# Squares of the late output tiles moved from VectorE to ScalarE, and their sum to TensorE, in a two-layer hybrid diffusion block

## The reference

```python
def rmsnorm(x, g):
    xf = x.astype(jnp.float32)
    y = xf * lax.rsqrt(jnp.mean(xf * xf, axis=-1, keepdims=True) + RMS_EPS)
    return (y * g.astype(jnp.float32)).astype(x.dtype)
...
y = jnp.concatenate([y_gla, y_four, y_conv], axis=-1) @ w_out
x = x + mod_lat[2] * rmsnorm(y_lat, g_mix_post[i])
...
h = modulate(rmsnorm(x, g_pre), shift, scale)
a, u = jnp.split(h @ w_ffn_in, 2, axis=-1)
y = (jax.nn.silu(a) * u) @ w_ffn_out
return x + gate * rmsnorm(y, g_post)
```

## Time and profile before

| what | value |
|---|---|
| median of 3 runs | 1631.08 us (1630.3 to 1632.72) |
| the profiled execution's own time | 1628.16 us |
| its span | 1626.4 us |
| TensorE busy | 1550.0 us, 95% of the span |
| VectorE busy | 845.3 us, 52% |
| ScalarE busy | 568.3 us, 35% |
| GpSimd busy | 589.6 us, 36% |

### The profile page before, as it was taken

How to read it: one execution, slowest core, us unless ns; L and a number is a source line. 1 busy time by engine, 2 the same in 40 slices (tenths; PEclk the granted TensorE clock), 3 DMA queues, 4 the chain that set the end, 5 groups by cost and what they waited for, 6 DMA issues and landing times.

```text
span 1626.4 us, 23073 instructions
## 1 busy us (share of the span) xinstructions
PE 1550.0 (95%) x9124; PEld 1385.0 (85%) x9124; DVE 845.3 (52%) x1361; ACT 568.3 (35%) x917; POOL 589.6 (36%) x309
## 2 busy tenths in 40 slices
PE   5998999999899999999999979999989999999997
PEld 2898999786799999999998769888877888888886
DVE  2576887746756326661466764366645321221137
ACT  4643214525444214441243255422424422231221
POOL 0531212245324524552355323331241544444441
PEclk9999999999999999999999999999999999999999
DMA  9444441255312212221123243432260323232321
GB/s 372 177 152 161 164 159 34 88 190 206 118 53 78 78 35 94 79 67 63 55 76 123 85 143 109 150 142 80 77 260 27 104 91 102 91 103 90 104 81 62
DMA packets 52910, 183.93 MB, mean 113 GB/s; under 512 B 5522, under 2 KB 10514, under 8 KB 48852
## 3 DMA queue, kind: packets, MB, share of 16 engines
q1 hardware_dynamic: 46674, 168.85, 29.3%
q10 hardware_dynamic: 6146, 13.83, 2.5%
HBM read 171.13 MB, written 11.53 MB: 112 GB/s over the span
## 4 chain that ended last, share of the span: by engine, by line
PE 81%; DVE 7%; DMA 4%; ACT 4%; issue 1%; POOL 1%; SPq 1%; ACTq 0%; DVEq 0%; POOLq 0%
PE A L1032 55%; PE A L1284 8%; PE N L1284 4%; PE G L1284 4%; DMA raw<-stream 2%; PE G L1339 1%; DMA raw<-modw 1%; DVE bg L1886 1%; PE G L1146 1%; DMA mraw<-modv 1%; PE A L1180 1%; PE G L1053 1%; DVE mraw L1888 1%; PE G L1187 1%; PE A L1218 1%
## 5 line engine op out<-in xcount | busy, mean ns | idle before, releaser
L970 POOL TENSOR_TENSOR w_lo<-raw,w_hi 128x1024 fp32r<-128x1024 f32 (+2 forms) x163 | 382.4, 2348 | 674.8 <-ACT w_hi L1366 637.8
L1032 PE MATMUL A<-h_hi,w_hi 128*128 128x512 f32 (+2 forms) x1264 | 414.3, 358 | 24.7 <-POOL h_lo L1015 12.9
L1032 PE MATMUL A<-h_hi,w_lo 128*128 128x512 f32 (+2 forms) x1264 | 403.7, 350 | 0.0
L1032 PE MATMUL A<-h_lo,w_hi 128*128 128x512 f32 (+2 forms) x1264 | 403.7, 350 | 0.0
L1366 ACT ACTIVATE w_hi<-raw 128x1024 fp32r<-128x1024 f32 (+2 forms) x163 | 167.2, 1028 | 388.8 <-PE A L1032 334.4
L1032 PEld LDWEIGHTS A<-h_hi,w_hi 128*128 128x128 f32 x1264 | 234.8, 190 | 72.6 <-POOL h_lo L1015 19.2
L1032 PEld LDWEIGHTS A<-h_hi,w_lo 128*128 128x128 f32 x1264 | 236.3, 190 | 21.8
L1032 PEld LDWEIGHTS A<-h_lo,w_hi 128*128 128x128 f32 x1264 | 236.7, 190 | 20.9 <-issue 0.5
L1032 PE MATMUL A<-g_hi,w_hi 128*128 128x384 f32 (+2 forms) x480 | 145.6, 346 | 3.8 <-DVE g_lo L1857 2.0
L1032 PE MATMUL A<-g_hi,w_lo 128*128 128x384 f32 (+2 forms) x480 | 144.4, 344 | 0.0
L1032 PE MATMUL A<-g_lo,w_hi 128*128 128x384 f32 (+2 forms) x480 | 144.4, 344 | 0.0
(11 more groups left out here) (313 smaller groups left out, 2656.1 us busy)
## 6 DMA issues: line engine op xcount, KB each, us to landing
raw<-stream SPq DMA_DIRECT2D x150, 512.0 KB, 3.3
mraw<-modv SPq DMA_DIRECT2D x48, 512.0 KB, 3.3
mraw<-modw SPq DMA_DIRECT2D x14, 1024.0 KB, 6.7
raw<-pairs SPq DMA_DIRECT2D x18, 512.0 KB, 4.6
raw<-modw SPq DMA_DIRECT2D x6, 1024.0 KB, 14.7
x<-x_keep ACTq DMA_DIRECT2D x4, 1536.0 KB, 13.2
raw<-stream SPq DMA_DIRECT2D x16, 384.0 KB, 3.0
mraw<-pairs SPq DMA_DIRECT2D x9, 512.0 KB, 3.2
```

The source lines that it names most:

```text
L970: pool.tensor_tensor(lo, like_chunk(n, raw[:, n % RAW, 0:WIDTH[n]]), hi.bitcast(F32), ALU.subtract).then_inc(lo_done, 1)
L1032: m = pe.matmul(dst[:, at:at + t1 - t0], a, b[:, k, t0:t1], start=(first and p == 0), stop=(last and p == 2))
```

## The change

The entry `take` now ends for VectorE with the copy or addition that brings the tile into `y`. ScalarE gets a part in `take`: it squares the tile from `y` into columns 512 to 767 of `sqs`, by turns in the two buffers. A new entry `tsq` m lets TensorE multiply that square by `one_d` and add it up in the bank N1, where the mean of part 1 is formed; `mean` of part 1 is the eighth matmul of that sum. `tsq` m stands two late tiles behind: m-2 follows late m, 6 stands just ahead of the mean, and the eighth is the mean itself. For each tail TensorE so gets 8 matmuls of this kind where it had 2.

```diff
--- before.py
+++ after.py
@@ -119,7 +119,11 @@
 
         nxt = (L, 1) if w == 0 else (L + 1, 0)
         more = nxt[0] < DEPTH
-        late = lambda m: order.append(("late", L, w, m))
+        def late(m):
+
+            order.append(("late", L, w, m))
+            if m > 1:
+                order.append(("tsq", L, w, m - 2))
         piece = lambda *ks: modk(1, w, () if w else ks)
 
         def steps(kind, s, ks):
@@ -168,6 +172,7 @@
             ahead(7)
             take(7)
             order.append(("head", L, w, 0, 0))
+            order.append(("tsq", L, w, 6))
             order.append(("mean", L, w, 1))
             piece(6)
             steps("res", 1, range(KT))
@@ -210,7 +215,7 @@
                 take(6)
                 steps("nrm", 0, range(3, KT))
                 take(7)
-                order.extend((("head", L, w, 0, 0), ("mean", L, w, 1), ("head", L, w, 1, 0)))
+                order.extend((("head", L, w, 0, 0), ("tsq", L, w, 6), ("mean", L, w, 1), ("head", L, w, 1, 0)))
                 steps("res", 1, range(KT))
                 order.append(("head", L, w, 2, 0))
                 steps("sq", 1, range(KT))
@@ -334,7 +340,17 @@
 
 def sums_before(L, w):
 
-    return KT * (4 * L + 2 * w)
+    return KT * (2 * L + w)
+
+
+def late_squares(L, w, m):
+
+    return (KT - 1) * (2 * L + w) + m
+
+
+def sum_event(e):
+
+    return e if e[0] == "mean" and e[3] == 0 else ("tsq",) + e[1:3] + (0,) if e[0] == "mean" else ("sq",) + e[1:4] + (0,)
 
 
 def span(e):
@@ -403,7 +419,9 @@
                 used["A1"] += KT // 2
             elif kind == "late":
                 units = [f"A{e[3] % 2}"]
-            elif kind == "mean" or kind == "sq" and e[4] == 0:
+            elif kind == "tsq" and e[3] == 0:
+                units = ["N1"]
+            elif kind == "mean" and e[3] == 0 or kind == "sq" and e[4] == 0:
                 units = ["G0" if kind == "sq" and e[1:4] == (1, 1, 1) else "G1" if kind == "sq" and e[3] == 0 else f"N{e[3]}"]
             self.before[e] = [(u, used[u]) for u in units]
             for u in units:
@@ -649,6 +667,7 @@
             sem("osq_ready"), sem("orstd_ready"), sem("yg_ready"), sem("yhi_ready"), sem("ylo_ready"))
         ssq_ready, rstd_ready, xnew_ready, sq_ready, sq_used = (
             sem("ssq_ready"), sem("rstd_ready"), sem("xnew_ready"), sem("sq_ready"), sem("sq_used"))
+        tsq_ready, tsq_used = sem("tsq_ready"), sem("tsq_used")
         haff_ready, hhi_ready = sem("haff_ready"), sem("hhi_ready")
         yn_ready, rstd_copied, half_done = sem("yn_ready"), sem("rstd_copied"), sem("half_done")
         hlo_ready_p, hlo_ready_v = sem("hlo_ready_p"), sem("hlo_ready_v")
@@ -723,7 +742,7 @@
 
         def sum_bank(e):
 
-            at = PLAN.before[e if e[0] == "mean" else ("sq",) + e[1:4] + (0,)][0][0]
+            at = PLAN.before[sum_event(e)][0][0]
             t0, t1, _ = span(e)
             return {"N0": N[:, 0:t1 - t0], "N1": N[:, 512:512 + t1 - t0], "G0": G[0][:, 0:t1 - t0],
                     "G1": G[1][:, 0:t1 - t0]}[at]
@@ -738,6 +757,10 @@
             s, k = e[3:]
             at = 256 * (1 + k // 2 % 2)
             return sqs[k % 2][:, at:at + CTX] if s else sqs[k % 2][:, 0:span(e)[1]]
+
+        def late_square(m):
+
+            return sqs[m % 2][:, 2 * CTX:3 * CTX]
 
         def scaled(e, j):
 
@@ -1322,13 +1345,19 @@
                 elif kind == "mean":
                     unit_free(e)
                     t0, t1, _ = span(e)
-                    sums = sums_before(L, e[2]) + KT * (e[3] + 1)
-                    pe.wait_ge(ssq_ready, sums - e[3])
-                    m = pe.matmul(sum_bank(e), one_d[:, :], ssq[:, t0:t1], start=True, stop=(e[3] == 0))
                     if e[3]:
-                        pe.wait_ge(ssq_ready, sums)
-                        m = pe.matmul(sum_bank(e), one_d[:, :], sil[:, t0:t1], start=False, stop=True)
+                        pe.wait_ge(tsq_ready, KT * (2 * L + e[2] + 1))
+                        m = pe.matmul(sum_bank(e), one_d[:, :], late_square(KT - 1), start=False, stop=True)
+                    else:
+                        pe.wait_ge(ssq_ready, sums_before(L, e[2]) + KT)
+                        m = pe.matmul(sum_bank(e), one_d[:, :], ssq[:, t0:t1], start=True, stop=True)
                     m.then_inc(full["mean"], 1)
+                elif kind == "tsq":
+                    w, m = e[2:]
+                    unit_free(e)
+                    pe.wait_ge(tsq_ready, KT * (2 * L + w) + m + 1)
+                    pe.matmul(sum_bank(("mean", L, w, 1)), one_d[:, :], late_square(m), start=(m == 0),
+                              stop=False).then_inc(tsq_used, 1)
                 elif kind == "sq":
                     s, k = e[3:]
                     t0, t1, _ = span(e)
@@ -1677,7 +1706,14 @@
                     if e[2] and e[3] == 0:
                         act.preload_act_table_set(LN_SET)
                     act.wait_ge(full["mean"], PLAN.full[e])
-                    normalise(e, e)
+                    normalise(e, sum_event(e))
+                elif kind == "take":
+                    w, m = e[2:]
+                    t0, t1, _ = parts(e)[1]
+                    read_out(act, ("late", L, w, m))
+                    if m > 1:
+                        act.wait_ge(tsq_used, late_squares(L, w, m - 1))
+                    act.activation(late_square(m), y[:, m, t0:t1], ACT.Square).then_inc(tsq_ready, 1)
                 elif kind == "sq":
                     s, k = e[3:]
                     t0, t1, _ = span(e)
@@ -2078,24 +2114,8 @@
                     at = t0 + L * SEQ // 2
                     ym, src = y[:, m, t0:t1], A[m % 2][:, at:at + t1 - t0]
                     dve.wait_ge(chunk_used, (TWICE[L, w] + m if (L, w) in TWICE else PLAN.n0[late]) + 1)
-                    square = N[:, 512:512 + t1 - t0]
-                    if m == KT - 1:
-
-                        out = dve.tensor_tensor(ym, src, ym, ALU.add) if w else dve.tensor_copy(ym, src)
-                        out.then_inc(free[f"A{m % 2}"], 1)
-                        read_out(dve, late)
-                        dve.tensor_tensor(sil[:, t0:t1], ym, ym, ALU.mult).then_inc(ssq_ready, 1)
-                        continue
-                    if w:
-                        dve.tensor_tensor(ym, src, ym, ALU.add).then_inc(free[f"A{m % 2}"], 1)
-                        read_out(dve, late)
-                        link(dve.tensor_tensor(square, ym, ym, ALU.mult))
-                    else:
-                        link(dve.tensor_copy(ym, src))
-                        dve.tensor_tensor(square, src, ym, ALU.mult).then_inc(free[f"A{m % 2}"], 1)
-                        read_out(dve, late)
-                    dve.wait_ge(ssq_ready, sums_before(L, w) + KT + m)
-                    dve.tensor_tensor(ssq[:, t0:t1], square, ssq[:, t0:t1], ALU.add).then_inc(ssq_ready, 1)
+                    out = dve.tensor_tensor(ym, src, ym, ALU.add) if w else dve.tensor_copy(ym, src)
+                    out.then_inc(free[f"A{m % 2}"], 1)
                 elif kind == "ffn_in" and L == 0:
                     for q in range(FAST):
                         if q == 3:
```

## The result

| kernel | median us (lowest to highest, runs) | ratio to the kernel before, 95% interval |
|---|---|---|
| before | 1631.85 (1629.55 to 1633.46, 8) | |
| the change | 1635.87 (1634.01 to 1637.34, 8) | 1.0024 [1.0013, 1.0035] |

What follows compares the result with a forecast made beforehand. TensorE was taken as the bound (95% of the span), with idle waits in the four tails. Tails +2.6 - 1.4 + 1.4 + 2.1 = +4.7 on 1628.16 gave 1632.9, plus 2.9 to the runs' median: 1635.8 us, range 1631.0 to 1640.5.

Steps and rivals of the forecast that it cites:

- (0,0), +2.6: Tail (0,0): new sums on TensorE's path, a wait for ScalarE and a norm-stage square add 2.6 us, between +1.7 and +3.5.
- The wait of 0.45: Tail (0,0): TensorE waits 0.45 us for the first square of x, behind tile 1's square and the rounding on ScalarE.
- (0,1) first half, -0.6: Tail (0,1) before the norm: the chain ends at 938.8 instead of 939.40, 0.6 us earlier, with the clock whole.
- I take it that the shorter wait leaves the clock whole: Tail (0,1): after a 1.9 us wait instead of 2.33, TensorE stays at full clock; otherwise 1.7 us more.
- The rival's +1.1: Tail (0,1): the clock falls after the new wait too, making the whole tail +0.3 instead of -1.4, 1637.5 us; chance 0.20.
- Its norm, -0.8: Norm stage of (0,1): VectorE loses a square of 1.12 and an addition of 0.42 us; half counted, 0.8 us gained.
- (1,0), +1.4: Tail (1,0): four new sums cost 1.7 us and the norm gains 0.3, in all +1.4, between 0 and +2.
- +1.7: Tail (1,0): the sums after late 3, 4, 5 and 6 lie on TensorE's path and cost 1.7 us.
- (1,1), +2.1: Tail (1,1): eight output-transfer issues of 3.7 us on ScalarE's queue hold back the last square, so the mean starts 2.1 us later.
- VectorE as the pace: Rival, all tails: TensorE stands waiting for VectorE between late tiles, so new sums cost nothing; -4.6 us, 1626.5; chance 0.08.
- Issues hidden: Rival, tail (1,1): the output-transfer issues don't hold back the last square; tail +0.6, sum +3.2, 1634.3 us; chance 0.17.
- TensorE pays for all: Rival, all tails: TensorE pays for nearly all new matmuls, 21 x 0.43 = +9.0 us, 1640.1; chance 0.05.

Runs made afterwards that it cites:

- doubled sums: The change with each of the seven sums of squares of late tiles issued twice on TensorE; ratio 1.0061 to the kernel before.
- both versions of VectorE's additions: The change with VectorE adding up ScalarE's squares one tile later, ratio 1.0007; the same with output transfers on SyncE and tile 1's square behind, 1.0003 (both to before).
- the last experiment: The kernel before plus 24 small ScalarE copies into a tile nothing reads, ahead of part 0's mean in (0,1); ratio 1.0050 to the kernel before.

## Why the prediction was right, and where it was not

The direction and most terms came out of the mechanism that was foretold; that the median fits to 0.1 us is luck, as the end of this list says.

- **Prices.** 377 ns a record and 0.43 us a product held on each chain; doubled sums cost 0.43 each where nothing waited.
- **(0,0), +2.6.** +2.8. The wait of 0.45 was 0.49. Undoing the order gave 0.7 back, so ScalarE's order cost a little more than that wait.
- **(0,1) first half, -0.6.** The step that failed is "I take it that the shorter wait leaves the clock whole". It fell in both executions of the change, and with the output transfers moved: +1.3. The rival's +1.1 was right. The row that had spoken for a whole clock was the wait of 2.42 us ahead of (1,0); the kernel before, run again, has the same 2.42 us there and the clock at 0.50 in the microsecond from 1194 us on. One row was no evidence. The Trainium skill ("TensorE: Matmul & The Clock Gate", section "Why this matters for your kernels") warns that idle gaps between bursts of matmuls set the clock back. This tail did that, but the gaps that the page names are longer than the 1.95 us here, so the prediction's "by the rule" asked more of the page than it states.
- **Its norm, -0.8.** -2.3: -1.1 from VectorE, near the term, and -1.0 to -1.4 from the stall behind the transfers' issue, which no step had.
- **(1,0), +1.4.** +0.7, by other parts than forecast. From the restart of TensorE behind the transfer to the norm's Ln it is 21.16 us with the four sums and 19.56 without them where the clock is whole (the version with the change in (0,1) alone): +1.6 for the +1.7. But the kernel before takes 21.16 too: behind its 3.34 us, and the 2.80 of its second execution, the clock fell, and behind the change's 1.34 and 1.23 it did not. The step "+1.7" left out that the clock there could change. And the restart itself comes 1.1 us later after the mixer's last Ln (43.7 us for 42.6), though the prediction had the long wait end at the same time. A chunk of weights lands later there. ScalarE's wait for it in before and in the change:

```profile
1181.34 1.06 ACT L1361 ACTIVATE h_hi<-raw 128x1024 fp32r<-128x1024 f32 x1 [8.10 <-DMA raw<-stream]
```

```profile
1188.26 1.06 ACT L1390 ACTIVATE h_hi<-raw 128x1024 fp32r<-128x1024 f32 x1 [9.42 <-DMA raw<-stream]
```

In all 14 executions the transfer is issued 7.4 us behind that Ln. In the eight with a q8 packet 11.1 to 12.3 us behind it, while the transfer runs, the chunk lands at 15.0 to 15.2 and TensorE restarts at 43.4 to 43.8; in the six whose packet falls outside, before and both versions of VectorE's additions among them, at 13.9 and 42.5 to 42.8. That the packet is the cause was not tried.

- **(1,1), +2.1.** +2.0. With the issues moved +0.6, the bound that was named.
- **Rivals.** VectorE as the pace: fell with the doubled sums. Issues hidden: fell. TensorE pays for all: fell, some 16 of the 24 new products lie on the path (four, three, four and five by tail). The clock: came true, and errors of the norm, with the other sign, hid it in the sum.
- **The sum.** Two errors, +1.9 us in (0,1) first and -1.5 in its norm, cancel but for 0.4, and -0.7 in (1,0) outweighs that. The forecast's +4.7 also stood on a median of 1631.1 for the kernel before, where 1631.85 was measured beside the change's 1635.87, so +4.0. That is luck twice.
- **The range.** Its ends don't follow from the bounds that are named for them: those of (0,0) and (0,1) give 1632.3 and not 1631.0, which needs (1,0) at 0 as well; the clock case with those of (0,0) and (1,1) gives 1639.3 and not 1640.5. And 0.67 for slower by over 0.2% is less than the parts named for it, which add up to about 0.8.

## What to carry to other kernels

The tails answered differently to one change: (0,1) became 1.0 us shorter, in part by the stall that fell away there, and the other three 0.7 to 2.8 us longer. So such a move is best made per stage, and beside the price of the moved instruction its place in the taking engine's queue counts: putting the output transfers on another queue, and one square behind another, gave back 1.4 and up to 1.9 us without any less work. Where a result is a few us, compare stretches between the same two instructions over repeated executions; most repeat within 0.1 us when two profiled executions of one kernel differ by 6.

## What was not expected of the hardware

- **The clock.** In (0,1), waits of TensorE of 1.47 to 1.64 us left it whole in six kernels, and in all eight executions with a wait of 1.95 to 2.70 us it went to half. Elsewhere the length doesn't decide: in (1,0) waits of 2.24 to 3.06 us left it whole in six kernels, and waits of 1.88, 2.80, 3.07 and 3.34 us didn't. A fall behind such a wait cost about 1.5 us.
- **Instruction packets.** Two issues of transfers on ScalarE's queue took 2.25 to 2.83 us where an instruction packet started 0.1 to 0.3 us behind the first, and 0.94 to 1.01 us in the ten executions where it started elsewhere. A 512 KB transfer of weights landed 1.1 to 1.3 us later where one fell into it. Adding or taking away TensorE's instructions far ahead moves such packets, so a stretch can change that the edit never touched.
- **Place of data.** In the last experiment the new tile of 96 bytes a partition shifts all tiles behind it. The groups of the FFN's matmuls, before and then with it, over 380 us:

```profile
L1032 PE MATMUL A<-g_hi,w_hi 128*128 128x384 f32 x256 | 65.0, 334 | 0.0
```

```profile
L1033 PE MATMUL A<-g_hi,w_hi 128*128 128x384 f32 x256 | 65.9, 339 | 0.0
```

Records are 1.5% longer, in this kernel alone: the mean is 334 ns in all 13 other executions. The 24 copies come only behind this stretch (at 909.5 us), so the moved tiles are the likely cause; that wasn't tried. The program is 8.2 us slower, and how much of that goes this way was not worked out.
